# Opening of a two-layer encoder kernel: the last square tile and one modulation slot each go to TensorE, and the second modulation sum gets a bank of its own

## What is computed

```python
m = jax.nn.silu(c) @ w_mod + b_mod               # modulation: shift, scale, gate
shift, scale, gate = jnp.split(m, 3, axis=-1)
h = _rmsnorm(x, norm_g[i]) * (1.0 + scale) + shift
proj = h @ w_in                                   # layer 0: z, bg, cg, xh
```

## Time and profile before

| | us |
|---|---|
| median of 3 runs | 811.7 |
| lowest, highest | 811.37, 811.87 |
| the profiled execution | 811.5 |
| its span | 809.7 |
| TensorE busy in the span | 801.4 (99%) |
| VectorE, ScalarE, GpSimd busy | 647.3, 443.0, 57.5 |

### The profile page before, as it was taken

One profiled execution on the slowest core, in us unless ns is written; L12 is line 12 of the kernel. 1 busy time (PEld: TensorE's weight loads), 2 busy tenths in 40 slices (PEclk: granted clock), 3 DMA queues, 4 the chain that ended last, 5 costly groups with the idle time before them and its releaser, 6 DMA issues.

```text
span 809.7 us, 15226 instructions
## 1 busy us (share of the span) xinstructions
PE 801.4 (99%) x5610; PEld 751.9 (93%) x5610; DVE 647.3 (80%) x948; ACT 443.0 (55%) x624; POOL 57.5 (7%) x76
## 2 busy tenths in 40 slices
PE   9999999999999999999999999999999999999997
PEld 8889999999999999988889888899999999988896
DVE  5989999998999899898654686567888888897534
ACT  4675666666666666562323843456667677762220
POOL 1010000000000000001100000010000000000000
PEclk9999999999999999999999999999999999999999
DMA  9996565657565656689422363414455445497103
GB/s 349 366 211 194 132 195 169 199 164 202 164 205 159 204 162 197 169 316 338 166 84 74 104 235 104 130 27 144 142 155 156 129 130 152 134 306 265 53 1 105
DMA packets 40175, 139.43 MB, mean 172 GB/s; under 512 B 4562, under 2 KB 6738, under 8 KB 40144
## 3 DMA queue, kind: packets, MB, share of 16 engines
q1 hardware_dynamic: 31760, 111.16, 38.3%
q0 software_dynamic: 7232, 25.69, 16.9%
q10 hardware_dynamic: 1152, 2.18, 0.7%
HBM read 109.13 MB, written 4.20 MB: 140 GB/s over the span
## 4 chain that ended last, share of the span: by engine, by line
PE 96%; issue 2%; DVE 1%; POOL 0%; POOLq 0%; DVEq 0%
PE pp L1211 11%; PE pp L1212 11%; PE pp L1213 11%; PE pp L1067 8%; PE pp L1068 7%; PE pp L1069 7%; PE p_aux L1211 7%; PE p_aux L1212 7%; PE p_aux L1213 7%; PE pp L1344 4%; PE pp L1342 4%; PE pp L1343 4%; PE pp L1166 3%; PE p_aux L1415 2%; PE pp L1083 1%
## 5 line engine op out<-in xcount | busy, mean ns | idle before, releaser
L1211 PE MATMUL pp<-h_hi,wh 128*128 128x256 f32 x280 | 79.3, 283 | 0.0
L1212 PE MATMUL pp<-h_lo,wh 128*128 128x256 f32 x280 | 79.2, 283 | 0.0
L1213 PE MATMUL pp<-h_hi,wl 128*128 128x256 f32 x280 | 79.2, 283 | 0.0
L1721 DVE TENSOR_TENSOR wl<-wt,wh 128x1024 fp32r<-128x1024 f32 x56 | 66.5, 1217 | 0.2 <-ACT wh L721 0.2
L721 ACT ACTIVATE wh<-wt 128x1024 fp32r<-128x1024 f32 x56 | 58.9, 1054 | 13.6 <-DVE wt L1702 7.6
L1211 PE MATMUL p_aux<-s_hi,wh 128*128 128x256 f32 x224 | 63.4, 283 | 0.0
L1212 PE MATMUL p_aux<-s_lo,wh 128*128 128x256 f32 x224 | 63.4, 283 | 0.0
L1213 PE MATMUL p_aux<-s_hi,wl 128*128 128x256 f32 x224 | 63.4, 283 | 0.0
L1211 PE MATMUL pp<-s_hi,wh 128*128 128x256 f32 x224 | 63.4, 283 | 0.0
L1212 PE MATMUL pp<-s_lo,wh 128*128 128x256 f32 x224 | 63.4, 283 | 0.0
L1213 PE MATMUL pp<-s_hi,wl 128*128 128x256 f32 x224 | 63.4, 283 | 0.0
(11 more groups left out here) (237 smaller groups left out, 2601.1 us busy)
## 6 DMA issues: line engine op xcount, KB each, us to landing
raw<-in_stream SPq DMA_DIRECT2D x144, 512.0 KB, 4.1
wl<-raw POOLq DMA_DIRECT2D x28, 512.0 KB, 4.5
raw_l<-in_stream SPq DMA_DIRECT2D x18, 512.0 KB, 5.1
raw_s<-in_stream SPq DMA_DIRECT2D x16, 512.0 KB, 13.4
wl_b<-raw POOLq DMA_DIRECT2D x16, 512.0 KB, 4.5
raw_m<-in_stream SPq DMA_DIRECT2D x14, 512.0 KB, 3.3
x_s<-in_xt SPq DMA_DIRECT2D x4, 512.0 KB, 5.9
w_lo_s<-raw POOLq DMA_DIRECT2D x4, 512.0 KB, 6.3
```

The lines of the kernel that those rows point to most:

```text
L1211: pe.matmul(out, hi, hi_of(k), start=fresh and k == 0, stop=False, skip_group_check=not fresh)
L1212: pe.matmul(out, hi, lo_of(k), start=False, stop=False, skip_group_check=not fresh)
L1213: mm = pe.matmul(out, lo, hi_of(k), start=False, stop=k == 3, skip_group_check=not fresh)
L1721: dve.tensor_tensor(wl[par][:, part], wt[par][:, part], f32(wh[par][:, part]), ALU.subtract).then_inc(t_cut, 1)
```

## The change

It has six parts.

1. The eighth tile of squares is no longer added by DVE: four matmuls of PE sum it straight from `x_sq` into `p_rstd`, and the four that sum `ssum` add to them. `SQ_START` goes from 7 to 6.
2. Sum 0: slots 0 and 1 are now summed by tiles on DVE (`kt` 0 to 3), and slot 2 is the direct one (`DIRECT_SLOT`), placed after the sums of squares.
3. Sum 1: its columns go to the bank of `p_pair[1]`. Its direct slot stays slot 0, and no longer waits for `amp_ready`. The first matmul that overwrites that bank (kp = 0, u = 1) waits for `amp_ready` of 2.
4. `WARM` goes from (28, 3, 2) to (25, 3).
5. On DVE the first `h_lo` moves ahead of tiles 2 and 3 of sum 1.
6. SP waits for `stat_sum` before the slots of sum 2, and for the new counts before those of sum 3.

```diff
--- before.py
+++ after.py
@@ -47,9 +47,9 @@
 X_STEPS = KD + 2 + 1
 SQUARES = KD + 2
 SQ_STEPS = 1 + 6 + 2
-SQ_START = 7
+SQ_START = 6
 FREE = 2
-WARM = (28, 3, 2)
+WARM = (25, 3)
 WARM_END = 5
 LEAD = 0
 AHEAD = 3
@@ -78,7 +78,8 @@
 W_ROUNDS = len(CUT_ORDER) // RING
 
 S_RING = 12
-S_DIRECT = (2, 1, 0, 0)
+S_DIRECT = (1, 1, 0, 0)
+DIRECT_SLOT = (2, 0)
 WIDE = 120
 WIDE_AT = 32
 
@@ -317,15 +318,22 @@
             n = 4 * kp + j
             return n % S_RING, 16 * (n // S_RING + 1)
 
+        def s_count(kp, j):
+
+            return 4 * kp + j + 1 - sum(S_DIRECT[:kp]) - (kp < 2 and j > DIRECT_SLOT[kp])
+
+        def wide(kp):
+            return (p_small, p_pair[1])[kp][:, WIDE_AT:WIDE_AT + 4 * WIDE]
+
         def small(kp):
 
             if kp < 2:
-                return [p_small[:, WIDE_AT + WIDE * t:WIDE_AT + WIDE * t + 1] for t in range(4)]
+                return [wide(kp)[:, WIDE * t:WIDE * t + 1] for t in range(4)]
             return [p_small[:, 4 * kp + t:4 * kp + t + 1] for t in range(4)]
 
         def small_pair(kp, first):
             if kp < 2:
-                return p_small[:, WIDE_AT:WIDE_AT + 4 * WIDE].rearrange("p (t e) -> p t e", e=WIDE)[:, first:first + 2, 0]
+                return wide(kp).rearrange("p (t e) -> p t e", e=WIDE)[:, first:first + 2, 0]
             return p_small[:, 4 * kp + first:4 * kp + first + 2]
 
         ALL = slice(0, S)
@@ -393,12 +401,12 @@
                     kp, j = int(what[1]), START_ORDER[:q].count(what)
                     slot = s_at(kp, j)[0]
                     if kp == 2:
-                        sp.wait_ge(sq_added, SQ_START)
+                        sp.wait_ge(stat_sum, 1)
                     if kp == 3:
-                        if j < S_DIRECT[0]:
-                            sp.wait_ge(direct_done, j + 1)
+                        if j == DIRECT_SLOT[0]:
+                            sp.wait_ge(direct_done, 1)
                         else:
-                            sp.wait_ge(s_used, j + 1 - S_DIRECT[0])
+                            sp.wait_ge(s_used, s_count(0, j))
                     sp.dma_start(raw_s[:, slot, :], stream[q, :, :]).then_inc(ms_in[slot], 16)
                 else:
                     n = CUT_ORDER.index(what)
@@ -1136,27 +1144,29 @@
                 pe.wait_ge(ms_in[slot], land)
                 for n in range(2):
                     for t in range(4):
-                        mm = pe.matmul(p_small[:, WIDE_AT + WIDE * t:WIDE_AT + WIDE * (t + 1)],
+                        mm = pe.matmul(wide(kp)[:, WIDE * t:WIDE * (t + 1)],
                                        raw_s[:, slot, S * n + P * t:S * n + P * (t + 1)], silu_w[:, 2 * j + n, :],
-                                       start=j == 0 and n == 0 and t == 0, stop=False, skip_group_check=True)
+                                       start=n == 0 and t == 0, stop=False, skip_group_check=True)
                 mm.then_inc(direct_done, 1)
 
 
             pe.wait_ge(consts, 3)
             keep_clock(WARM[0])
-            pe.wait_ge(wide_ready, 1)
-            direct_columns(0, 0)
+            pe.wait_ge(sq_ready, KD)
+            for st in range(NCH):
+                pe.matmul(p_rstd[:, st:st + 1], x_squared(KD - 1)[:, P * st:P * (st + 1)], ones[:, 0:1],
+                          start=st == 0, stop=False, skip_group_check=True)
             pe.wait_ge(sq_added, SQ_START)
             for st in range(NCH):
-                mm = pe.matmul(p_rstd[:, st:st + 1], ssum[:, P * st:P * (st + 1)], ones[:, 0:1], start=True, stop=True)
+                mm = pe.matmul(p_rstd[:, st:st + 1], ssum[:, P * st:P * (st + 1)], ones[:, 0:1],
+                               start=False, stop=True, skip_group_check=True)
             mm.then_inc(stat_sum, 1)
-            direct_columns(0, 1)
             keep_clock(WARM[1])
+            pe.wait_ge(wide_ready, 1)
+            direct_columns(0, DIRECT_SLOT[0])
             broadcast(p_rstd[:, :], 2, ALL)
             start_columns(0)
-            keep_clock(WARM[2])
-            pe.wait_ge(amp_ready, 1)
-            direct_columns(1, 0)
+            direct_columns(1, DIRECT_SLOT[1])
             for kp in range(4):
                 w = (0, 1, 3, 4)[kp]
                 pe.wait_ge(hi_cut, CUT_ORDER.index(w) + 1)
@@ -1186,6 +1196,8 @@
                 w = (2, 5)[kp // 2]
                 pe.wait_ge(*low_made(w))
                 for u in range(2):
+                    if kp == 0 and u == 1:
+                        pe.wait_ge(amp_ready, 2)
                     for n in range(2):
                         k = 2 * kp + n
                         at = slice(256 * (k % 4) + P * u, 256 * (k % 4) + P * (u + 1))
@@ -1497,7 +1509,7 @@
                 a, w = acc_s[:, kp % 2, :], raw_s[:, slot, S * n:S * (n + 1)]
                 if n == 0:
                     dve.wait_ge(ms_in[slot], land)
-                if kt > 2 * S_DIRECT[kp]:
+                if kt > (0, 2, 0, 0)[kp]:
                     dve.wait_ge(*start_at)
                     ins = dve.scalar_tensor_tensor(out=a, in0=w, scalar=silu_c[:, kt:kt + 1], in1=a,
                                                    op0=ALU.mult, op1=ALU.add)
@@ -1507,7 +1519,7 @@
                     start_at[:] = dve_step, step(ins)
                 else:
                     ins.then_inc(s_used, 1)
-                    start_at[:] = s_used, 4 * kp + kt // 2 + 1 - sum(S_DIRECT[:kp + 1])
+                    start_at[:] = s_used, s_count(kp, kt // 2)
 
             def start_tiles(kp, *kts):
                 for kt in kts:
@@ -1596,22 +1608,22 @@
 
             dve.wait_ge(sc_ready, 1)
             dve.tensor_copy(silu_w[:, :, :], silu_c[:, :].unsqueeze(2).broadcast_to([P, KD, WIDE])).then_inc(wide_ready, 1)
-            for k in range(1, KD):
+            for k in range(1, KD - 1):
                 dve.wait_ge(sq_ready, k + 1)
                 if k > 1:
                     dve.wait_ge(sq_added, k - 1)
                 dve.tensor_tensor(ssum[:, :], ssum[:, :] if k > 1 else x_squared(0), x_squared(k),
                                   ALU.add).then_inc(sq_added, 1)
-            start_tiles(0, 4)
+            start_tiles(0, 0, 1)
             dve.wait_ge(stat_sum, 1)
             rsqrt(1, p_rstd[:, 0:NCH], 1.0 / D, NCH)
-            start_tiles(0, 5, 6)
+            start_tiles(0, 2, 3)
             dve.wait_ge(power_ready, 1)
             for st in range(2, 4):
                 ins = dve.tensor_scalar(work[:, 0, P * st:P * (st + 1)], ident[:, :], rstd[:, st:st + 1], None,
                                         ALU.mult)
             ins.then_inc(diag_ready, 1)
-            start_tiles(0, 7)
+            start_tiles(0, 6, 7)
 
             def start_amp(kp):
                 dve.wait_ge(acc_used, kp + 1)
@@ -1636,8 +1648,8 @@
             start_amp(0)
             scale_tile(1, p_rstd[:, :], ALL, 0)
             cut_lo_start(0)
+            cut_h_tile(0, 0, ALL)
             start_tiles(1, 2, 3)
-            cut_h_tile(0, 0, ALL)
             start_tiles(1, 4)
             cut_h_tile(0, 1, ALL)
             start_tiles(1, 5, 6, 7)
```

## The result

| | median us | lowest to highest | executions |
|---|---|---|---|
| before | 811.61 | 811.01 to 814.6 | 22 |
| the change | 813.21 | 811.44 to 815.9 | 22 |

The ratio is 1.0022, with a 95% interval of 1.0015 to 1.0029: the change makes the kernel **slower**, by 1.6 us of medians where 0.8 us of gain were forecast. It also spreads the executions, from 811.44 to 815.9, where twenty of the 22 of the kernel before lie between 811.01 and 812.16. The profiled execution of the change took 814.36 us with a span of 812.4.

The account below looks back on a forecast made before the run. The prediction took matmuls to bound the kernel behind the opening, where PE's and DVE's chains bring h; of 1.37 us earlier at the first h matmul, 0.8 arrives: 811.7 - 0.8 = 810.9 us, range 810.0 to 812.1.

Parts of the forecast that it names:

- What bounds the kernel: Opening: two nearly equal chains, PE's and DVE's, up to weight slot 2; a gain has to pass both.
- from `amp` to slot 2: DVE, 8.65 us of full work; PE starts weight slot 2 at 26.2, not 27.05, so 0.8 to 0.85 arrives.
- Squares, variance, broadcast, `amp`: Opening: variance at 12.55, 1.20 us earlier; broadcast at 15.10; `amp` at 17.43, 0.81 us earlier.
- first h: PE's first matmul with h: could start at 19.4 instead of 20.77, 1.37 us earlier.
- The power: POOL, between variance and broadcast: stays at 1.40 us; rival of 1.97 us gives 811.5, chance 12%.
- the clock, given 4%: Rival, opening: with less filler the clock falls to 1.2 GHz at a hole near 15 us; 813.9 us, chance 4%.
- L / 2: Clock rival: cost of a stretch of length L at 1.2 GHz; with L of 6 us, 3 us.
- a later load takes the gain: Rival: addition of weight slot 5 still lands at 44.66, PE waits 1.15 instead of 0.35 us; 811.7, chance 15%.
- the moved `h_lo` changes the order, not the sum: DVE between `amp` and weight slot 2: moving `h_lo` leaves the 8.65 us of work the same.
- The new wait on `amp_ready` 2: PE, behind six matmuls at 27.57: costs nothing, since DVE is done by 27.31; without that cover 1.1 us.

Follow-up runs that it names:

- wide_hold_amp: wide_hold with the wait on `amp_ready` put back ahead of the direct slot of sum 1; median 810.80 us, ratio 0.9992 to the kernel before.
- wide: gated with the 16 passes for the sums of squares using 120 moving columns of ones instead of one; median 811.93 us, ratio 1.0005 to the kernel before.
- gated: The changed kernel with 27 matmuls of ones instead of 25, the last three groups held until 3, 5 and 7 squares are ready; median 812.68 us.
- after_hold: The changed kernel with SP's first main-loop load held until the low part of weight slot 4 is added; median 811.80 us.
- wide25_hold: wide_hold without the gates, its 25 matmuls of ones in one piece as in the changed kernel; median 810.83 us, ratio 0.9988 to the kernel before.
- before_warm14: The kernel before with 14 instead of 28 matmuls of ones ahead of its first direct slot; median 816.15 us, ratio 1.0052 to the kernel before.
- wide_hold: wide with SP's first main-loop load held until the low part of weight slot 4 is added; median 810.81 us, ratio 0.9993 to the kernel before.
- wide_hold_order: wide_hold with part 5 undone, the first `h_lo` again behind tiles 2 and 3 of sum 1; median 810.60 us, ratio 0.9990 to the kernel before.
- before_hold: The kernel before with SP's first main-loop load held until the low part of weight slot 4 is added; median 811.09 us, ratio 0.9996.
- fill33: The changed kernel with 33 instead of 25 matmuls of ones ahead of the sums of squares; median 811.72 us, ratio 1.0004 to the kernel before.

## Why the prediction was wrong, point by point

**What bounds the kernel.** Right. DVE from `amp` to slot 2 and PE were the two chains, and DVE's ends last (wide_hold_amp). Where PE waits for it was read wrong: I had PE end the columns of sum 1 at 25.8 and then stand in front of slot 2. In the wide kernel its weight loads stand 0.9 us in front of these columns, for DVE's last tile of sum 1, and 0.17 in front of slot 2.

**Squares, variance, broadcast, `amp`.** Right as a mechanism, where the clock holds. In the wide kernel: variance 12.60 (12.55 forecast), broadcast 15.16 (15.10), `amp` 17.44 (17.43), first h 19.05 (19.4, of which 0.24 is the chain's count against the timeline's), slot 2 at 26.34 (26.2). The power took 1.41 in the change, the 1.40 that I kept. None of that is what the changed kernel shows, for two reasons.

**First failed step: the clock, given 4%.** The prediction said "the rise is at 8.0, before the removed matmuls (10.46), and the holes add up to under 1 us". It took the rise of one execution for a property of the kernel. In the twelve other traces it came between 4.5 and 7.5 us. A block of ones is a count of passes and not a time: with a rise at 4.5 it is through at 8.93, and the hole is 2.03 us. And it counted one-column passes as work that keeps the clock; gated against wide, and after_hold against wide25_hold, show that the clock fell with them and, but for one execution, not with 120 columns in their place. Its price was too high as well: L / 2 would be 1.7 us for the usual 3.4 us at 0.50 (four traces; that of the change had 6.8, that of before_warm14 10.2). after_hold has the fall without the load's wait and is at 811.80, wide_hold without both, in the same group, at 810.81: about **1.0 us**. Half of L was too much because only a part of it lay on the chain: in gated the variance still came at 12.60, as in wide; behind it the direct slot took 3.14 us instead of 2.02, and `amp` came 1.0 us later (18.43 against 17.44).

**Second failed step: "a later load takes the gain".** The mechanism was close, the place wrong. I looked at slot 5, where PE had waited 0.35 us, and asked only whether its end would follow its issue. It came faster in the changed kernel's traces (5.6 and 5.7 us against 6.8), and just that released the load that ran beside the addition of slot 4, which had no wait in the trace before. I had not looked at who waits for slot 5 on SP. Price **1.4 us** (813.21 to 811.80 with the hold, medians of different groups), on a term that I had at nothing.

**Third, small: "the moved `h_lo` changes the order, not the sum".** It put tile 4 straight behind tile 3, and each tile needs the result of the one before. The row of two at 23.61 above takes 1.61 us. Undone, 0.2 us come back, by the traces and by the medians (810.81 to 810.60 in different groups).

**The new wait on `amp_ready` 2** cost nothing, as forecast: no trace shows a wait there. The range (810.0 to 812.1) missed since it held either of the two losses (after_hold 811.80, wide 811.93), and not both.

With the first two repaired the profiled execution has a span of 808.8 (wide_hold), with all three 808.6 (wide_hold_order), against 809.7 before. That this looks like the forecast 0.8 is in part luck. At slot 2 wide_hold is only 0.55 us earlier than before (26.39 against 26.94); the rest is the 0.35 us that PE waited for slot 5 in the trace before, a wait that the prediction meant to stay. before_hold's trace has no such wait, and against it the gain is 0.4 us of span (809.2 to 808.8) and 0.28 of medians.

What stays open: why slot 5's addition takes 5.7 us in some executions and 6.3 to 6.8 in others. fill33 and gated issue it at 38.18 and 38.22 us, behind SP loads that land at the same times. Open too is how much one-column work, behind how much idle time, lets the clock fall. The kernel before has executions near 811.0 and near 811.8; before_hold has all ten within 810.99 to 811.52, which fits a race of the same kind, but no trace of the kernel before above 811.5 was taken. The parts of the change were not tried one by one on the kernel before.

## What to carry to other kernels

Filler is sized in passes, but its length depends on when the clock rises, which differs from one execution to the next: tie it to the progress of what it waits for, or make it long enough for the early rise, and give the small sums near it a wide moving operand, which here cost no time. A mean clock that differs in the third digit between executions is worth following up in the stretches of the trace; by itself it also counts the low end of a kernel. When one transfer becomes faster or earlier, look at which load that releases and whose transfer it then runs beside; a trace that shows no wait there says nothing of the margin.

## What the runs showed of the hardware

- Eight passes with one moving column and eight with 120 take nearly the same time at full clock (0.81 to 1.01 us and 0.96 to 0.99 us to the next), but behind 16 of the first kind the granted clock fell from 1.00 to 0.50 at 12.7 us with TensorE's row busy (gated), and behind 16 of the second kind it did not (wide). Behind 16 of the first kind with 10 us of gapless ones ahead of them it did not fall either (fill33). The Trainium skill (TensorE: Matmul & The Clock Gate, What's actually happening) says that the block that sets the clock watches how busy the engine has been; the runs agree in that the clock fell behind idle time (before_warm14) or one-column passes (gated), and they add that a busy row in the profile does not tell what that block sees.
- The clock rose at 4.5 to 8.0 us, read from the spacing of the matmuls, behind the same first matmul at 1.68 us, in thirteen traces whose TensorE work is the same up to there.
- The addition of slot 4, 512 KB by a DMA of POOL, took 4.7 to 5.6 us with the load held (six traces), and 6.9 to 7.8 us with one load of 512 KB issued 0.30 to 0.35 us behind it (five traces).
- A stretch of 3.4 us at 0.50 cost about 1.0 us of the kernel's time (811.80 in after_hold, 810.81 in wide_hold).
